# Two transformer layers on one core: norms by half rows, rows normalised inside a product, and a first pair of experts with its own order

## The reference, cut to what matters

```
h = rms_norm(x, g_pre1) * (1 + sc1) + sh1
a = token_mix(h)                       # one input projection, three attention branches, gates, w_out
x = x + g1 * rms_norm(a, g_post1)
h = rms_norm(x, g_pre2) * (1 + sc2) + sh2
scores = sigmoid(h @ router_w)         # 64 experts, groups, top 6 of each token
moe = sum over chosen experts of gate * (silu(h @ Wg) * (h @ Wu)) @ Wd   + shared expert
x = x + g2 * rms_norm(moe, g_post2)
```

## Time and profile before

| | us |
|---|---|
| median of 3 runs | 1719.44 (1718.69 to 1720.09) |
| the profiled execution | 1719.05 |
| its span in the trace | 1717.2 |
| PE busy in the span | 1671.3 (97%) |
| DVE busy | 432.0 |
| ACT busy | 321.0 |

### The profile page before, as it was taken

One profiled execution on the slowest core, in us unless ns is written; L12 is line 12 of the kernel. 1 busy time (PEld: TensorE's weight loads), 2 busy tenths in 40 slices (PEclk: granted clock), 3 DMA queues, 4 the chain that ended last, 5 costly groups with the idle time before them and its releaser, 6 DMA issues. The chain is left out here.

```text
span 1717.2 us, 20998 instructions
## 1 busy us (share of the span) xinstructions
PE 1671.3 (97%) x8091; PEld 894.8 (52%) x8091; DVE 432.0 (25%) x1179; ACT 321.0 (19%) x754; POOL 121.2 (7%) x161
## 2 busy tenths in 40 slices
PE   6999999989999999999999999999899999999997
PEld 4778788543333333333367878884333333333332
DVE  1114444351111111111131444434311111111113
ACT  1010341121111111111120113402111111111111
POOL 3001000010000000001020000001100000000000
PEclk8999999999999999999999999999999999999999
DMA  9994233369999999999999632334899999999993
GB/s 388 397 407 155 87 110 129 123 233 405 424 424 424 426 425 426 425 425 425 420 392 420 263 108 98 101 137 161 305 415 427 425 426 425 423 427 423 426 426 136
DMA packets 60381, 559.87 MB, mean 326 GB/s; under 512 B 12941, under 2 KB 13089, under 8 KB 20353
## 3 DMA queue, kind: packets, MB, share of 16 engines
q1 hardware_dynamic: 45360, 529.55, 75.0%
q0 software_dynamic: 14928, 29.02, 4.9%
HBM read 576.02 MB, written 4.78 MB: 338 GB/s over the span
## 5 line engine op out<-in xcount | busy, mean ns | idle before, releaser
L1038 PE MATMUL PS<-ring,region 128*64 128x512 f32 x2048 | 450.6, 592 | 1.9 <-issue 1.5
L1038 PEld LDWEIGHTS PS<-ring,region 128*64 128x64 f32 x2048 | 147.3, 137 | 290.7 <-issue 290.6
L617 PE MATMUL PS<-region,ring 128*128 128x256 f32 x1088 | 245.4, 381 | 0.5 <-DMA ring<-in_blocks 0.5
L1085 PE MATMUL PS<-region 128*128 128x512 f32 x512 | 241.0, 594 | 0.0
L1062 PE MATMUL PS<-ring,region 128*64 128x512 f32 x1024 | 235.5, 602 | 0.2
L617 PEld LDWEIGHTS PS<-region,ring 128*128 128x128 f32 x1088 | 203.8, 190 | 34.2 <-issue 6.3
L1757 DVE SCALAR_TENSOR_TENSOR region<-region,PS 128x256 f32<-128x256 f32 x64 | 26.9, 421 | 670.6 <-ACT region L1320 670.6
L510 PEld LDWEIGHTS PS<-const,region 128*128 128x128 f32 (+1 forms) x925 | 106.8, 141 | 121.8 <-issue 74.1
L510 PE MATMUL PS<-const,region 128*128 128x128 f32 (+1 forms) x925 | 138.5, 279 | 18.2 <-DMA region<-in_c 8.7
L1062 PEld LDWEIGHTS PS<-ring,region 128*64 128x64 f32 x1024 | 68.1, 137 | 158.7 <-issue 158.0
L1324 ACT ACTIVATE region<-PS 128x512 f32<-128x512 f32 x128 | 76.4, 597 | 267.4 <-PE PS L1062 267.4
(11 more groups left out here) (260 smaller groups left out, 985.4 us busy)
## 6 DMA issues: line engine op xcount, KB each, us to landing
ring<-in_expert_blocks SPq DMA_DIRECT2D x192, 2048.0 KB, 16.7
ring<-in_blocks SPq DMA_DIRECT2D x120, 1024.0 KB, 19.7
region<-post_rows POOLq DMA_DIRECT2D x8, 512.0 KB, 5.3
h_table<-region POOLq DMA_DIRECT2D x4, 512.0 KB, 4.0
region<-in_w_kvk POOLq DMA_DIRECT2D x2, 640.0 KB, 18.2
region<-in_mla_w_ukv POOLq DMA_DIRECT2D x2, 512.0 KB, 21.4
region<-in_post_pack POOLq DMA_DIRECT2D x2, 512.0 KB, 24.7
region<-h_table,region POOLq DMA_INDIRECT x64, 10.7
```

The costliest lines, as they stand in the source:

```text
L617: last = pe.matmul(PS[:, j % 2, m * T:(m + 1) * T], w[:, k, m * P:(m + 1) * P], hT[:, k, :], start=(k == 0), stop=(k == KC - 1))
L1038: last = pe.matmul(PS[e * CAP:(e + 1) * CAP, 0, :], xe[:, k, e * CAP:(e + 1) * CAP], w[:, k % 4, :], start=(k == 0), stop=(k == KC - 1), s ...
L1085: last = pe.matmul(PS[:, 4 + 2 * t + half, :], hot[:, t * P:(t + 1) * P], og[:, half * HALF:(half + 1) * HALF], start=False, stop=True, sk ...
```

## The change

The edits:

1. Sums of squares are made for half rows: two instructions of 512 columns with a sum each (`SUMS` is 16), each released when its half is there. `x_ready` and `x1_ready` count halves.
2. `normalise_x` is gone. DVE writes root times identity into a 128x128 tile (`root_diagonal`), and `normalised` runs `pe.matmul(xr chunk, diagonal)` in place of the transpose. The product transposes and scales at once.
3. `add_normalised` becomes `take_gains` (PSUM times gains, by halves, before the root is known) and `add_rows` (residual plus rows times root, by halves).
4. At the start of layer 1 and at each layer's end, one `both_roots` (nine instructions on 128x2) stands in place of two `row_root`.
5. `normalised(1, 0)` moves into the last half of the output projection, after its fourth step. ACT squares tile 1's second half only after modulating tile 0. The slots that `normalised(1, 0)` released are now released by `router(0)`.
6. `shared_gate_up(0)` runs six steps before `normalised(1, 1)` (three before), one before the router of tile 1 and one before the logits; `shared_gate_up(1)` runs six steps before the ranks.
7. POOL writes the rows of h2 into two tables. The first pair's gather reads the one without gates and no longer waits for the gates; PE gets the first pair's gates by one more product in `first_tokens`, which `first_gate` holds. The gather of pair 1 waits for the gate columns.
8. The first pair's `gate_up` waits for its inputs by halves, and `transpose_lists` stands in it after two of eight steps. `transpose_inputs(1, 0)` goes ahead of `transpose_hidden(0)`, `transpose_inputs(1, 1)` ahead of `down(0)` and into bank 3.
9. `shared_down(0)` is split around `shared_transposes(1)`.
10. At the end the sums start by halves of the last `combine`, four stores by halves replace three, and POOL's addition is gone. The last pair's slots are released by ACT.

```diff
-                def normalised(call, t, src, bank, frees=0):
+                def normalised(call, t, diag, bank, frees=0):
                     pe.wait_ge(xn_ready, l * 4 + (2 * call + t + 1))
                     for c in range(KC):
-                        last = transpose(PS[:, bank + c // 4, (c % 4) * P:(c % 4 + 1) * P], src[:, t, c * P:(c + 1) * P])
+                        last = pe.matmul(PS[:, bank + c // 4, (c % 4) * P:(c % 4 + 1) * P], xr[:, t, c * P:(c + 1) * P], diag[:, t, :],
+                                         start=True, stop=True)
...
+                            if t == 1 and half == 1 and k == 3:
+                                normalised(1, 0, diag2, 0)
...
-                normalised(1, 0, xn2, 0, frees=2)
-                router(0)
+                router(0, frees=2)
...
-                shared_gate_up(0, range(3))
-                normalised(1, 1, xn2, 6)
-                shared_gate_up(0, range(3, 5))
+                shared_gate_up(0, range(6))
+                normalised(1, 1, diag2, 6)
+                shared_gate_up(0, range(6, 7))
                 logits(0)
                 router(1)
-                shared_gate_up(0, range(5, 6))
+                shared_gate_up(0, range(7, KC))
                 logits(1)
-                shared_gate_up(0, range(6, KC))
...
+                    for t in range(2):
+                        last = pe.matmul(PS[:, 1, 2:4], first_hot[:, t, :], h2x[:, t, D:D + 2], start=(t == 0), stop=(t == 1), skip_group_check=True)
+                    last.then_inc(first_done, 1)
...
+                            if g == 0 and k % 4 == 0:
+                                pe.wait_ge(xe_ready, done + (k // 4 + 1))
+                                if g == 0 and k == 2 and e == 0:
+                                    transpose_lists()
...
-                    transpose_lists()
                     gate_up(0)
+                    transpose_inputs(1, 0)
                     transpose_hidden(0)
-                    transpose_inputs(1, 0)
+                    transpose_inputs(1, 1)
                     down(0)
-                    transpose_inputs(1, 1)
...
+                    pool.dma_start(first_table[P * t:P * (t + 1), :], h2x[:, t, 0:D]).then_inc(table_in, 16)
+                    pool.dma_start(table[P * t:P * (t + 1), 0:D], h2x[:, t, 0:D]).then_inc(gates_in, 16)
...
-                pool.wait_ge(table_in, (l + 1) * 64)
+                pool.wait_ge(table_in, (l + 1) * 32)
...
+                def root_diagonal(r, t, diag):
+                    ve.tensor_scalar(diag[:, t, :], ident, r, ROOT_SCALE, ALU.mult, ALU.mult).then_inc(xn_ready, 1)
+                def take_gains(i, t, rows, rows_in):
+                    dve.wait_ge(postb_in, (l * 2 + rows_in) * 2 * 16)
+                    for half, cols in enumerate(HALVES):
+                        dve.wait_ge(sum_done, l * SUMS + 2 * i + half + 1)
+                        step.add(ve.tensor_tensor(rows[:, t, cols], PS[:, 4 + 2 * t + half, :], postb[:, t, cols], ALU.mult))
+                def add_rows(r, t, rows, done):
+                    for half, cols in enumerate(HALVES):
+                        ve.scalar_tensor_tensor(out=xr[:, t, cols], in0=rows[:, t, cols], scalar=r, in1=xr[:, t, cols], op0=ALU.mult, op1=ALU.add).then_inc(done, 1)
...
-            pool.tensor_tensor(xr[:, 0, :], xr[:, 0, :], moe_scaled[:, 0, :], ALU.add).then_inc(last_ready, 1)
```

More of the change, by code:

```diff
@@ L925, in router @@
                                          start=(k < 2), stop=(k >= KC - 2), skip_group_check=True)
+                        if k == 0 and frees:
+                            release(last, frees)
                     last.then_inc(router_done, 1)
@@ L961, in shared_down @@
                     pe.wait_ge(htok_ready, l * 4 + 2 * t + 2)
-                    for half in range(2):
+                    for half in parts:
                         for f in range(2):
@@ L1058, in down @@
                         for half in range(2):
+                            if g == 0 and half:
+                                pe.wait_ge(xe_ready, done + 4)
                             for f in range(2):
@@ L1328, in _ @@
                     half_tanh(0)
-                    take_inputs(1, 0)
+                    for half in range(2):
+                        take_inputs(1, half)
                     for half in range(2):
                         take_out(0, half)
-                    take_inputs(1, 1)
                     for g in range(1, PAIRS):
```

189 lines of the change are left out of this document (104 added, 85 removed).

## The result

| | before | after |
|---|---|---|
| median, us | 1719.43 (1718.69 to 1720.09) | **1709.55** (1709.21 to 1710.37) |
| ratio to before | | 0.9943, 95% interval 0.9927 to 0.9959 |
| the profiled execution | 1719.05 | 1709.25 |
| its span | 1717.2 | 1706.6 |

The change wins 9.9 us; the forecast was 1710.3. Part 1 of the page of the kernel after stands against the earlier trace rows: PE is busy as long as before (80 more instructions, but between 16 and 1700 us only 3.4 us at the lower clock, before 13.6), and the span shrank around it.

A forecast was written before the change was run, and what follows sets the result against it. PE, busy 1671.3 of 1717.2 us, bounds the kernel, with the weight stream saturated too. Terms 0 - 2.4 + 0.35 - 4.5 - 2.6 = -9.15 take 1719.05 to 1709.9; median forecast 1710.3, range 1708 to 1712.5.

The forecast's parts named there:

- Added work: Each normalised grows from 8 to 16 instructions, 0.9 to 1.75 us: plus 0.87, four times per layer, 7.0 in all.
- Projection to pair 1, layer 0: From output projection to pair 1's gate_up: 3.55 us earlier, or -3.05 with the 0.5 added before the last pair.
- Layer 0 behind the stream: At layer 1's last modulation step, PE could be 3.05 us earlier, weight blocks only 2.4: -2.4, bounds 0 and -3.05.
- a wait of 1 us or more: Sign of being right: PE waits this long for a ring block before layer 1's last modulation step.
- Start of layer 1: PE's own 32 instructions follow the last block and feed the projection later: +0.35 us, bounds 0 and +1.75.
- Layer 1: Projection to pair 1 gains 5.2 with the clock held, stream allows 5.0, less 0.5: -4.5 us, bounds -3.4 and -4.9.
- End: Last additions done at 1712.1, not 1714.78: -2.6 us, 2.0 of it one stalled root step; bounds -2.0 and -3.0.
- The rule on POOL's fill: Shared SBUF interfaces: POOL's fill of xg, now over the second tile's root, would hold it by up to 2.0 us.
- The stream does not move: Rival, 20%: layer 0's PE gain becomes a longer wait for the block at 870.68; -4.15 in all, 1715.3 us.
- The first gather gains nothing: Rival, 8%: pair 0's gather queues behind the gate columns, 0.4 us too late, which the list hides; 1710.4 us.
- everything follows: Rival, 10%: all gains carry through and the waits shrink more; 1705.8 us.
- The slower case: Rival, 6%: pair 1's gather comes late, PE idles and its clock falls in both layers; +3.65, 1723.1 us.

The follow-up runs named there:

- e5: Kernel after the change with half the bytes of every expert load (outputs not the reference's): 1708.93 us, ratio 0.9942.
- e6: Kernel before the change with half the bytes of every expert load (outputs not the reference's): 1718.90 us, ratio 0.9998.
- e1: Kernel after with the product form undone, DVE scaling whole rows and PE transposing them: 1705.47 us, ratio 0.9918 to before.
- e12: e1 with, in layer 0, the lists transposed at step 3 and ring slots given back at step 6, so a later load: 1706.64 us.
- e3: Kernel after with one table again, the first gather waiting for the gate columns and bringing the gates: 1711.69 us, ratio 0.9957.
- e10: e1 with hidden transposes ahead of pair 1's input transposes and, in layer 0, the lists at step 3: 1712.46 us.
- e7: Kernel after with the first pair in its old order and half the bytes of every expert load: 1719.46 us, ratio 0.9997 to before.
- e9: Kernel after with the first pair in its old order and unread identity products filling PE's waits: 1715.31 us, ratio 0.9979 to before.

## Why the prediction was right, and where its sizes were off

- **Sum.** Forecast for the profiled execution 1709.9, measured 1709.25; for the median 1710.3, measured 1709.55. By the span the gain was 10.6, the sum 9.15: two terms were 0.7 and 1.0 too small, both beyond their own bounds (-5.20 against -4.9, -3.39 against -3.05). The time around the span, which no term holds, took 0.8 back. That the number came out within 0.8 us is in that part luck.
- **Added work.** 16 instructions were to take 1.75 with the end left off: the next group starts 1.78 us after 335.46 (337.24). Right. The start of layer 0 was to cost 0 and cost 0.05.
- **Projection to pair 1, layer 0.** Forecast -3.55, measured -3.21. `router(0)` at 340.77 with 1.09; `normalised(1, 1)` at 347.88 (forecast 347.75); first tokens 362.81 (362.7), after 0.24 of idle time instead of 0.5; `gate_up(0)` 372.27 (372.3); lists 374.98 (374.85). From there the forecast was 0.4 short: it ran the last six steps from the lists' start and left out the 0.24 us of their transposes. The hidden rows kept their 2.06, now as 0.49 + 0.66 + 0.92 us. The idle time ahead of the lists was 0.78, where the sign named 0.5. The gather of pair 1 was faster than thought (4.2 instead of 5.6 us).
- **Layer 0 behind the stream: the step that was wrong.** "PE could be 3.05 earlier at 870.68, the blocks only 2.4." The blocks came 3.39 earlier, PE only 2.8 (869.51 to 866.72). The argument took the DMA share of 1.01 for a stream that moves only as far as its first loads go out earlier and idle DMA time is filled. The stream moved farther: the sign "a wait of 1 us or more" did not come, the wait fell from 1.17 to 0.57. e5 and e6 show how little it bound: from `gate_up(1)` to this point halving the bytes is worth 0.75 us in after and 1.35 in before, and nothing in the loop. The margin of 1.1 us that the prediction read from the 791.2 load was no cap either: e1 has `gate_up(1)` 4.7 us ahead of before and goes through the loop at 15.13 us a pair. A limit exists, but farther off: e12, with `gate_up(1)` 6.1 us ahead of before and one load given out later, is the kernel that reached it.
- **Start of layer 1.** Forecast +0.35, measured +0.43.
- **Layer 1.** Forecast -4.5, measured -5.20 (5.61 less 0.41 behind it). The clock stayed up, as said, and pair 1 gained 5.6 instead of 5.2; a stream cap of 5.0 was not there. The bound of -4.9 does not follow from the prediction's own terms: 5.2 less 0.5 is 4.7. PE waited 0.93 us for the gather of pair 1, close to the 1 us named as a sign of being wrong.
- **End.** Forecast -2.6, measured -2.47; each root step takes under 0.2 us without POOL's addition. No run puts the addition back alone, so that it was the cause of the 2.22 us step rests on the two traces.
- **The rule on POOL's fill.** The fill ran at 341.00 for 2.83 us over the root steps from 342.21 on; they kept 0.15 to 0.22 us. The fill did not hold DVE.
- **The rivals.** "The stream does not move" fell (0.57 us of wait, not more than 1.17). "The first gather gains nothing" is false in layer 1 only (e3). The sum of "everything follows" takes off 0.35 that its terms do not hold; without it it gives 1706.1. The slower case, a late gather of pair 1, did not happen in the change, but e10 made it happen: there the load that follows it decides (e12), not the table's third write. It has the two parts that the rival named, latency and then the clock. Of the 6.3 us at `gate_up(1)` of layer 0 against e1, some 4.0 is latency and some 2.3 the clock, by the 5.04 us that e12 takes from the same gather to `gate_up(1)` where e10 takes 7.31; the rival had 1.7 for the clock.
- **What was missing.** The prediction priced the product form at 0.87 us a tile and looked only for what hid it. Its own numbers had the cheaper choice: DVE had 4.4 us to spare at `normalised(1, 0)`, and scaled rows would have cost PE no added instruction. The change is 4.1 us slower than it could be (e1).

Open: what sets the arrival of layer 1's last modulation block. From the last instruction of the last `combine` it takes 7.2 to 8.7 us in the kernels with full loads, and PE's own start explains only part of that (e1 and e12 have the last `combine` at the same time, and the block 1.2 us apart).

## What to carry to other kernels

Where PE waits for a short chain on other engines at a phase change, order its remaining work so that the wait falls into pieces; here that was worth 6.5 of 9.9 us, and with the old order useless products in the waits gave 3.5. Folding a scaling into a product did not pay here, where the engine that had done it was mostly in time: price the added PE instructions against the wait they remove, tile by tile. A saturated DMA share doesn't say that the stream binds; halve the bytes and see.

## What the runs showed of the hardware

- A float32 product with 128 moving columns is two instructions of 0.11 us, a transpose of the same chunk one: 32 instructions (16 products) took 3.74 us, 8 transposes 1.04.
- PE's clock went to its lower level after a single wait of 2.06 us (before, layer 1: down products 5.30 us instead of 3.65) or 2.16 (e10, layer 1), and in e12 at 868.8 after waits of 0.21, 1.41 and 0.51 us; with the same 2.06 us it held in layer 0 of before. In the first pair of layer 1 it cost 1.3 to 1.8 us each time. In layer 0 of e7, with two stretches at the lower level, `gate_up(0)` to `gate_up(1)` took 19.53 us instead of 15.05. With products of the identity in the waits it stayed up (e9).
- A gather whose issue was followed by a 2 MB load 0.47 us later could be used just behind that load, 9.0 us after issue; with 1.31 and 2.2 us between them it took 4.4 and 4.3. The Trainium skill, DMA: Bandwidth & Descriptors, section Queues, rings and completion order, says that each DMA engine takes turns between its queues packet by packet. From 380 us on e10 agrees roughly (51 packets of the gathers' queue, small ones among them, beside 56 of the loads'), and so the queue with the smaller packets gets few bytes. The 3 us before, in which the gather did not move, are not explained by it.
